# Who moves the first half's residual, and in what order two half-layers hand over: one change to a one-core transformer block

## The reference

```python
h = rmsnorm(x, norm_mix_pre);  y = mixer(h, ...)        # ends in y @ w_out
x = x + rmsnorm(y, norm_mix_post)
h = rmsnorm(x, norm_ffn_pre);  y = conv_mlp(h, ...)     # w_up (1024 x 5632), w_down (2816 x 1024)
x = x + rmsnorm(y, norm_ffn_post)
```

## Time and profile before

| | |
|---|---|
| median of 3 runs | 1877.07 us (1871.8 to 1877.71) |
| profiled execution, own time | 1876.34 us |
| its span, first to last instruction | 1874.5 us |
| mean granted TensorE clock | 0.993 of full speed |
| PE busy | 1816.4 us, 97% of the span |
| DVE busy | 1202.6 us, 64% |
| POOL busy | 716.9 us, 38% |
| ACT busy | 607.1 us, 32% |
| DMA | 170.81 MB, mean 91 GB/s |

### The profile page before, as it was taken

How to read it: one execution, slowest core, us unless ns; L and a number is a source line. 1 busy time by engine, 2 the same in 40 slices (tenths; PEclk the granted TensorE clock), 3 DMA queues, 4 the chain that set the end, 5 groups by cost and what they waited for, 6 DMA issues and landing times.

```text
span 1874.5 us, 20822 instructions
## 1 busy us (share of the span) xinstructions
PE 1816.4 (97%) x8516; PEld 1488.6 (79%) x8516; DVE 1202.6 (64%) x1117; ACT 607.1 (32%) x750; POOL 716.9 (38%) x296
## 2 busy tenths in 40 slices
PE   6999999998999999999999999999999999999996
PEld 5778888886888888888888887777778888888784
DVE  6454677847797777777754566754466666666534
ACT  4233222254300000000123333411256656565621
POOL 5456555543135445445444345244421111201152
PEclk9999999998999999999999999999999999999998
DMA  4233222144322222222444355412311111102232
GB/s 165 103 111 102 79 79 79 45 147 135 113 90 68 79 67 67 73 83 68 137 156 151 118 174 174 157 37 76 103 38 34 35 45 34 33 23 68 85 124 90
DMA packets 58285, 170.81 MB, mean 91 GB/s; under 512 B 6592, under 2 KB 6976, under 8 KB 58208
## 3 DMA queue, kind: packets, MB, share of 16 engines
q1 hardware_dynamic: 41456, 122.18, 20.8%
q10 hardware_dynamic: 16752, 47.56, 6.7%
HBM read 131.44 MB, written 38.27 MB: 91 GB/s over the span
## 4 chain that ended last, share of the span: by engine, by line
PE 84%; DVE 7%; ACT 4%; issue 3%; DMA 1%; POOL 1%; ACTq 0%; DVEq 0%; SPq 0%
PE psum L550 40%; PE psum L810 9%; PE psum L908 6%; PE psum L574 5%; PE psum L929 5%; PE psum L866 4%; PE psum L965 4%; PE psum L731 3%; PE psum L918 3%; PE psum L891 1%; DVE ptl L1876 1%; ACT pth L1380 1%; PE psum L677 1%; DMA xr<-xT 1%; PE psum L590 1%
## 5 line engine op out<-in xcount | busy, mean ns | idle before, releaser
L461 POOL TENSOR_TENSOR wh<-wstage,ones 128x1024 fp32r<-128x1024 f32 x92 | 223.7, 2432 | 800.1 <-PE psum L550 379.4
L466 POOL TENSOR_TENSOR wl<-wstage,wh 128x1024 fp32r<-128x1024 f32 x134 | 348.5, 2603 | 199.5 <-ACT wh L1030 182.1
L550 PE MATMUL psum<-hh,wh 128*128 128x512 f32 x1184 | 372.0, 395 | 20.0 <-POOL wl L466 15.6
L550 PE MATMUL psum<-hl,wh 128*128 128x512 f32 x1184 | 366.1, 390 | 0.0
L550 PE MATMUL psum<-hh,wl 128*128 128x512 f32 x1184 | 365.5, 390 | 0.0
L550 PEld LDWEIGHTS psum<-hh,wh 128*128 128x128 f32 x1184 | 220.6, 188 | 72.5 <-issue 26.8
L550 PEld LDWEIGHTS psum<-hl,wh 128*128 128x128 f32 x1184 | 223.0, 188 | 46.9
L550 PEld LDWEIGHTS psum<-hh,wl 128*128 128x128 f32 x1184 | 222.9, 188 | 46.9
L1756 DVE SCALAR_TENSOR_TENSOR cc<-uu,col,cc 128x1023 f32<-128x1023 f32 x88 | 187.9, 2135 | 3.1
L1765 DVE TENSOR_TENSOR al<-ain,ah 128x512 fp32r<-128x512 f32 x44 | 103.0, 2351 | 87.3 <-ACT ah L1251 87.3
L1239 ACT ACTIVATE cc<-cc 128x1024 f32<-128x1024 f32 x22 | 23.3, 1061 | 374.2 <-DVE cc L1756 374.2
(11 more groups left out here) (275 smaller groups left out, 3324.6 us busy)
## 6 DMA issues: line engine op xcount, KB each, us to landing
wstage<-w_units SPq DMA_DIRECT2D x163, 512.0 KB, 3.6
acts<-cc ACTq DMA_DIRECT2D x22, 512.0 KB, 2.6
ain<-acts SPq DMA_DIRECT2D x44, 256.0 KB, 3.8
resid<-yo SPq DMA_DIRECT2D x32, 256.0 KB, 2.4
mix<-spill ACTq DMA_DIRECT2D x12, 512.0 KB, 2.6
xin<-xT ACTq DMA_DIRECT2D x8, 512.0 KB, 8.7
kq<-mix SPq DMA_DIRECT2D x16, 256.0 KB, 3.9
gates<-gspill ACTq DMA_DIRECT2D x8, 512.0 KB, 2.6
```

The lines of the kernel that those rows point to most:

```text
L461: pool.tensor_tensor(high, wstage[:, u % STG], ones[:, :].unsqueeze(1).to_broadcast([P, 8, P]), ALU.mult).then_inc(w_high, 1)
L466: pool.tensor_tensor(low, wstage[:, u % STG], high.bitcast(F32), ALU.subtract).then_inc(w_split, 1)
L550: mm = pe.matmul(out[:, t], w[:, wslot, b, :], x[part][:, xk, t], start=start and n == 0, stop=stop and n == 2)
```

## The change

1. SP no longer moves the residual tiles of half 0. ScalarE's queue issues store and load behind each tile's high part and square. SP loads weight units U_OUT + 5 to U_FF + 5 without a break, then the moves of half 1.
2. In the out-projection's half 1, ScalarE and VectorE take the residual tiles of half 0 in pairs (0,1), (2,3), (4,5), (6,7), one pair between two out tiles. VectorE adds the squares of out tiles (1, 4) to (1, 6) after the last pair.
3. The fifth unit of both `next_layer` calls goes by halves: half 0 waits for the root that was read from bank 0, half 1 for the emptied bank 1.
4. At the end of the down-projection's half 0 all banks are emptied first, then the squares are made. The sum of squares moves on TensorE from behind k = 1 to the middle of k = 2. Half 1's order of emptying stays.

```diff
@@ block.sync
-            for u in range(U_OUT + 5, U_FF):
+            for u in range(U_OUT + 5, U_FF + 6):
                 load_unit(u)
-            for k in range(KT):
-                move_residual(1, 0, k, xT, resid1)
-                if k in (0, 2, 4, 5):
-                    load_unit(U_FF + (0, 2, 4, 5).index(k))
-            load_unit(U_FF + 4)
-            load_unit(U_FF + 5)
@@ block.tensor
+            def fifth_unit(base, rooted, emptied):
+                pe.wait_ge(w_split, base + 5)
                 for half in range(2):
-                    mm = half_products(bank(half), place(U_FF + 4), k, half, k == 0, k == KT - 1)
-            mm.then_inc(unit_done, 1)
+                    pe.wait_ge(*(emptied if half else (root_ready, rooted)))
+                    for k in range(KT):
+                        mm = half_products(bank(half), place(base + 4), k, half, k == 0, k == KT - 1)
+                mm.then_inc(unit_done, 1)
+            fifth_unit(U_FF, 3, (up_evac, 1))
@@ down-projection on block.tensor
-                    if k:
+                    if half and k == 2:
+                        down(1, 2, range(4))
+                        pe.wait_ge(y_odd, 4)
+                        sum_half(0, KT - 1, (acc_step, 12 + 6), (fsq_ready, KT))
+                        down(1, 2, range(4, KT - 1))
+                    elif k:
-                    if half and k == 1:
-                        pe.wait_ge(y_odd, 4)
-                        sum_half(0, KT - 1, (acc_step, 12 + 6), (fsq_ready, KT))
...
-            for j in range(4, len(L0_SLOTS)):
+            fifth_unit(U_L0, 5, (evac, E_L0 + 1))
+            for j in range(5, len(L0_SLOTS)):
@@ block.scalar
             def high_tiles(*tiles):
                 for k in tiles:
                     residual_tile(1, 0, k, C_FPRE)
+                    act.dma_start(resid1[k, :, 0:HT], yo[:, k, 0:HT]).then_inc(res_out, DMA)
+                    if k + 2 < KT:
+                        act.dma_start(xr[:, k % 2, 0:HT], xT[k + 2, :, 0:HT]).then_inc(xr_in[k % 2][0], DMA)
...
             out_tile(1, 1)
-            high_tiles(0)
+            high_tiles(0, 1)
+            weight_high(U_OUT + 14)
             out_tile(1, 2)
-            weight_high(U_OUT + 14)
-            high_tiles(1, 2)
+            high_tiles(2, 3)
             out_tile(1, 3)
-            high_tiles(3)
             weight_high(U_OUT + 15)
-            high_tiles(4)
+            high_tiles(4, 5)
             out_tile(1, 4)
             weight_high(U_FF)
-            high_tiles(5, 6)
+            high_tiles(6, 7)
             out_tile(1, 5)
             weight_high(U_FF + 1)
-            high_tiles(7)
             out_tile(1, 6)
             weight_high(U_FF + 2)
             weight_high(U_FF + 3)
             out_tile(1, 7)
...
+                for m in range(0, KT, 2):
+                    taken(m)
+                    if half and m < 6:
+                        squared(m // 2)
+                for m in range(3 if half else 0, KT):
                     squared(m)
@@ block.vector
             low_tiles(0, 1)
             out_added(1, 1)
-            low_tiles(2)
+            low_tiles(2, 3)
             out_added(1, 2)
-            low_tiles(3)
+            low_tiles(4, 5)
             out_added(1, 3)
-            low_tiles(4, 5)
-            out_added(1, 4)
-            low_tiles(6)
-            out_added(1, 5)
-            low_tiles(7)
-            out_added(1, 6)
+            low_tiles(6, 7)
+            for m in range(4, KT - 1):
+                out_added(1, m)
...
+                for m in range(1, KT, 2):
+                    taken(m)
+                    if half and m in (3, 5):
+                        added(m // 2)
+                for m in range(3 if half else 1, KT - 1):
                     added(m)
```

More of the change, by code:

```diff
@@ L790, in ff_unit @@
                 unit(slot(j % 4), (j + 2) % RING, H)
-            pe.wait_ge(w_split, U_FF + 5)
-            pe.wait_ge(up_evac, 1)
-            for k in range(KT):
+            def fifth_unit(base, rooted, emptied):
+                pe.wait_ge(w_split, base + 5)
                 for half in range(2):
-                    mm = half_products(bank(half), place(U_FF + 4), k, half, k == 0, k == KT - 1)
-            mm.then_inc(unit_done, 1)
+                    pe.wait_ge(*(emptied if half else (root_ready, rooted)))
[3 more added lines that the diff above has]
+            fifth_unit(U_FF, 3, (up_evac, 1))
             with pe.Fori(0, 3) as i:
```

## The result

| | before | after |
|---|---|---|
| median | 1875.5 us (1871.8 to 1877.71, 4 runs) | 1862.27 us (1861.03 to 1866.85, 4 runs) |
| ratio of after to before | | 0.9936, 95% interval 0.9911 to 0.996 |
| profiled execution | 1876.34 us | 1866.85 us, span 1865.0 |
| clock | 0.993 | 0.996 |

The change is faster, by 13.2 us in these medians and 9.5 us between the two profiled executions. The kernel before has one execution more than in its first table (1873.93), taken beside the kernel after.

The account below looks back on a forecast made before the run. TensorE was taken as the bound, with 8.7 us of wait at L582 the only large one in the edited parts. Terms -4.7 + 0 + 0 from 1876.34 gave 1871.6 us; range 1865.8 to 1876.4 with 8 in 10, its own 1869.1 to 1874.4.

Parts of the forecast that it names:

- What bounds: TensorE busy 97%; in the edited parts the only large wait is 8.7 us at L582, plus 1.8 us lost clock.
- Parts 1 and 2: Out-projection half 1: ScalarE moves the residual, tiles in pairs; L582's wait goes, gain 4.7 us.
- What is late next: Chain from U_FF + 1's high part to out tile (1, 7)'s square ends at 454.9; TensorE waits 4.3 us at L599.
- The issue itself: ScalarE's queue: each transfer issue takes 0.5 us, partly hidden; 0.3 us taken per tile, 1.0 if nothing hides them.
- The path between the tiles: Residual tiles of half 0: each next add follows an xr load landing after 4.8 us; tile 7 added at 441.5.
- From tile 7 on: U_FF + 1's high part starts at 444.7, after a correction for the old order; the square of (1, 7) ends at 454.9.
- The clock: TensorE behind the new wait at L599: the clock drops and costs 1.7 us.
- The wait goes for good: Rival, chance 0.17: U_FF + 1's high part by 441.5, about 1 us idle, clock up; gain 9.6, without wait 10.7.
- Transfers share and stretch: Rival, chance 0.15: transfers in two queues stretch xr landings to 6.3 to 6.5 us; gain 0.9, 1875.4 us.
- ScalarE's queue holds TensorE up: Rival, chance 0.08: ScalarE's work waits behind 14 issues and out tiles behind pairs; 4.0 us slower, 1880.3.
- Part 3: Fifth unit by halves in both next_layer calls: zero, the gain bounded by the 1.4 us wait behind cq.
- Part 4: Down-projection's half turn: sum 2.7 us later, covers of 1.3 and 0.4 us hold; zero, or up to 1 us loss.

Follow-up runs that it names:

- e4: Kernel before with only the halved fifth units and the down-projection's banks first, late sum: 1876.35 us, ratio 0.9997 to the kernel before.
- e8: Kernel before with only ScalarE moving the residual and tiles in pairs: 1866.48 us, ratio 0.9949 to the kernel before.
- e2: Kernel before with only the residual moved to ScalarE's queue, tiles in the old order: 1869.51 us, ratio 0.9958 to the kernel before.
- e7: Changed kernel, but SP moves the residual, its weight loads behind tiles 2, 4, 6 and 7: 1864.88 us, ratio 0.9941 to the kernel before.
- e3: Kernel before with only the tiles in pairs, SP still moving the residual between weight loads: 1881.4 us, ratio 1.0026 to the kernel before.
- e1: The changed kernel run again on another chip: 1866.49 us against 1876.98 for the kernel before, ratio 0.9942.
- e5: Changed kernel, but ScalarE issues a tile's store and load only when its square is done: 1867.2 us, ratio 0.9949 to the kernel before.
- e6: Changed kernel with out tile (1,7) ahead of U_FF + 3's high part on ScalarE: 1864.29 us, ratio 0.9933 to the kernel before.
- e14: The changed kernel as it is, on another chip: 1864.34 us, ratio 0.9936 to the kernel before (1876.79).
- e12: Kernel before, GpSimd's split of U_L0 + 12 waiting for VectorE's three cq low parts: 1872.70 us, ratio 0.9977 to the kernel before.
- e13: Changed kernel, GpSimd's split of U_L0 + 12 waiting for VectorE's three cq low parts: 1861.69 us, ratio 0.9922 to the kernel before.

## Why the prediction was wrong, point by point

- **What bounds: right.** The 8.65 us wait was the only place where the change gave anything (e4, e8), and its price with the clock, 10.5 us, was right: with 0.9 us of new wait taken off it gives 9.6, and the chain moved by 9.66.
- **Parts 1 and 2, the step that failed.** "What is late next" forecast a wait of 4.3 us at the second sum and 1.7 us of clock behind it; 0.89 us and no clock were measured. It put the square of out tile (1, 7) at 454.9, and that ended at 451.3, 3.6 us earlier. The mechanism was right (place, releaser, the fixed chain), its terms were not:
  - *The issue itself.* The load of `xr` for tile 2 was put beside the tile's own square, at 416.1; it went out at 414.43, and for tile 4 at 419.93 and not 423.8. The row at 376.15 was read for the one activation ahead of the transfer, and not as a queue running ahead of several. So tile 2's add came ahead of GpSimd's operation, by half a microsecond (418.84 against 419.31), and ended at 419.52 and not 422.6.
  - *The path between the tiles.* The forecast let each pair hang on the landing of a load, taken at 4.8 us beside a weight load; they took 3.1 to 3.7 and gated nothing. VectorE was the path, 7.8 us for a pair. So of the 3.1 us won at tile 2 only 1.7 are left at tile 7, whose add ended at 439.8 and not 441.5.
  - *From tile 7 on.* 0.75 us had been added because the arithmetic came out early for the old order; it was not needed. The high part of U_FF + 1 began at 441.96 and not 444.7. The chain from there to the square took 9.35 us and not 10.2, with the last weight load landing in 3.73 and not 4.4.
- **The clock.** The forecast took 1.7 us of clock on top of the wait, and 0.89 us of idle time cost none. A miss of 3.6 us in one time thus became 3.4 + 1.7 = 5.1 us in the sum: 4.7 forecast, 9.66 measured at that place. The 1.7 itself came from one place of before with 2.58 us of idle time; other traces have such places that cost nothing (below).
- **The rivals.** "The wait goes for good" named U_FF + 1 at 441.5, the square at 451.7, 1 us idle, the clock up, gain 9.6. That is what happened within 0.5 us, and it had 0.17. "Transfers share and stretch" was wrong here, as the `xr` loads landed in 3.1 to 3.7 us and not in 6.3. The forecast had set a rule beside it: by the Trainium skill (DMA: Bandwidth & Descriptors, Issuing engines are not separate DMA queues) issuing from several engines saves only the sequencer's time. The measurement decides: the move alone gave 7.5 us (e2), and SP's queue in another order gave as much as ScalarE's (e7), so the gain lay in the place in the order and not in the number of issuing engines. "ScalarE's queue holds TensorE up" did not happen with the early loads, but e3 is its mechanism on SP's queue: pairs that wait for a load carry the out tiles with them, 4.4 us slower.
- **Part 3: right**, zero; the 1.4 us behind `cq` stayed (e4, e8).
- **Part 4: right to the tenth.** The rows of after at the turn, TensorE, ScalarE and VectorE (answers to the earlier trace rows, 9.66 us earlier throughout):

```profile
1063.40 1.02 PE L591 MATMUL psum<-root,ones 128*128 128x512 f32 x2
```

```profile
1065.32 0.69 ACT L1034 ACTIVATE root<-psum,epsc 128x512 f32<-128x512 f32 x1 [5.58 <-PE psum L593]
1068.14 1.06 ACT L1031 ACTIVATE wh<-wstage 128x1024 fp32r<-128x1024 f32 x1 [2.13 <-PE psum L808]
```

```profile
1066.04 3.35 DVE L1503 RECIPROCAL rstd<-root 128x512 f32<-128x512 f32 x1 [5.09 <-ACT root L1034]
1069.75 5.28 DVE L1761 TENSOR_TENSOR al<-ain,ah 128x512 fp32r<-128x512 f32 x2 [0.36 <-ACT ah L1253]
```

  The sum is 2.7 us later than its shift, the root and reciprocal use up the cover down to the forecast 0.4 us (0.36), and ScalarE's next step is at 1077.80 - 9.66 = 1068.14.
- **The range.** The forecast's own came from bounds on the landings (gains of 2.6 to 7.2); the wide one ended at 1865.8, inside the first rival's 1865.6 to 1866.7. The scatter of the executions, 6 us in the runs shown, was called scatter and not looked into. Most of it was the two levels of the contest. On a chip at the upper level the change came to 1866.49, inside the range.

## What to carry to other kernels

When a transfer moves to a compute engine's queue, place it at the time when its own waits are met, not behind the engine's work ahead of it. In a queue that mixes moves others wait for with loads that must wait themselves, read each item's place before asking whose queue it is; grouping consumers without freeing that order cost this kernel 4.4 us (e3). When a time hangs on whether a short wait costs clock, give both outcomes real weight. And where executions of one kernel lie on two levels, find the place that tells them apart before comparing medians of three or four.

## What the runs showed of the hardware that was not expected

- VectorE and GpSimd, starting within 0.30 us of each other on SBUF tiles, hold each other up by whole operations. Once GpSimd's one took 6.06 us in place of 2.62, longer by about what VectorE's three take (3.49). Once VectorE's three took 7.87 us, 4.4 longer, while GpSimd did two operations (2.62 and 3.25). GpSimd's row starts first in both cases, so the start does not tell who is held up. It differs between the traces and, going by the times, between executions of one kernel and between chips. The Trainium skill (GPSIMD Engine Reference, Key points) says that GpSimd shares its SBUF interfaces with VectorE, with contention where a VectorE instruction has two SBUF inputs. The rows agree, as L1861 has two.
- The same idle time does not always cost clock. Behind 2.58 us of idle time at `gspill`, 96 products took 23.62 us in after and about that in before, e1, e4, e5 and e6, but 22.06 in e14 and 22.04 in e3, at the full pace. e2 lost nothing behind 2.50 us at the first sum, while e5 lost 1.6 us of clock behind 2.63 at the second. What TensorE did just before was the same in e1 and e14. What decides stays open.
- So the contest is worth 4.1 us on the kernel before (e12), wait and clock, and 2.7 on the one after (e13 against e14), whose traced execution had the wait alone.
